# Distances of keys from TensorE for the one-hot rows of a product-key stage, and a tail of two stages

## The chip, the cores and the metric

The kernel runs on one core of a Trainium2 chip. The metric is the device time of one execution in microseconds (us), from the first to the last instruction with the launch around it; lower is better. Engines: TensorE (PE, its weight loads PEld), VectorE (DVE), ScalarE (ACT), GpSimd (POOL), and SyncE (SP), which here issues every DMA.

## The reference

256 tokens of width 1024 pass through three blocks: pooling with retention, a chunked linear recurrence (HGRN), and a block that joins RWKV-7 and latent attention. Each is followed by a product-key expert layer ("PEER"). The last steps are a per-layer embedding with a gate, and an RMS norm.

```python
def peer_ffn(h, w_q, sub_keys, expert_u, expert_v):      # per block of 128 tokens
    q = (hb @ w_q).reshape(n, HEADS, 2, 128)
    s = einsum('nhcd,hckd->nhck', q, sub_keys)
    sc, ix = top_k(s, 16)                                 # 16 of 128 keys on each side
    cand = sc[:, :, 0, :, None] + sc[:, :, 1, None, :]
    top, pos = top_k(cand.reshape(n, HEADS, 256), 16)     # expert = 128 * first key + second key
    eidx = ...
    gate = softmax(top)
    act = gelu(einsum('nhed,nd->nhe', expert_u[eidx], hb))
    return einsum('nhe,nhed->nd', gate * act, expert_v[eidx])

x = x + peer_ffn(rmsnorm(x, g_ffn), ...)                  # third of the three PEER layers
x = x + (p @ w_ple_proj) * sigmoid(rmsnorm(x, g_ple) @ w_ple_gate)
return rmsnorm(x, g_final)
```

## The kernel before, in words

**Experts without a gather.** `peer` (L430) does not gather. It multiplies all tokens with all 16384 experts, 128 at a time, and weights each product with a gate that is zero where the expert was not chosen. For one token the 128x128 table of gates is a product of two matrices over the 128 choices (8 heads x 16): row n of A holds the choice's weight at its first key, and row n of B holds 1 at its second key. G = A^T B.

**The select part.** TensorE makes queries and key scores (L568, L579), ScalarE copies them out, and VectorE finds the top 16 on either side and of the pairs (`halves`, `pairs`, `store`). Beside this, TensorE multiplies the first 16 rows of the u table, whose high and low parts ScalarE and GpSimd split (`early_scores`, banks 6 and 7 of PSUM). The four residual matmuls (L626), which start the accumulation in banks 0 to 3, stand between the last keys and the early scores 6 to 15. VectorE then leaves in `c.sel` the first keys, the second keys and the weights, tokens on partitions. TensorE transposes all three (L634) to `c.selt`, choices on partitions.

**The gates.** The 256 tokens go in 64 quads of four. For quad g:

- VectorE makes A in four `tensor_scalar` (L920): iota equal to the key of the choice, times its weight. A lies in four buffers, which are `c.h`.
- B is made by turns, after the string `MAKER`: by VectorE in one `tensor_tensor` (L917, letter D), by GpSimd in four `tensor_scalar` (L1005, P), or by ScalarE in four Abs and one Relu (L751, L754, A).
- TensorE multiplies the four pairs (L652) into bank 4 + g % 4. A wait on `dve_moved` keeps it from a bank that is not yet emptied.
- ScalarE copies 112 columns of each token to G (L760). VectorE multiplies the other 16 into `held`, the activations that the early scores left (`gate_held`, L910), two quads behind.

SP loads v rows 0 to 2 before this, one of them into `c.spare`. After the last quad but one is gated, TensorE does the first scores of the long loop, and then the held outputs (`output_tile`, L606), for which VectorE and ScalarE split `held` and the v rows (L769, L932 to L936). ScalarE's `held_high(1)` writes `vh[:, 1]`, which is the memory of the second half of `c.h`. The loop over the remaining 112 rows follows.

**The clock of stages.** Each `stage(...)` is a block: all engines finish it before any starts the next one. Loads given to `c.prefetch` are issued by SP at the start of the next stage, and `first_tile` waits for them.

**The tail.** After the third `peer` (`second_block`, L2723) nine stages follow: `take_banks` (L1011), a load of `pt`, `product` (L1180) for the projection, `rms_scale` (L1705) and `transposes` (L132) within `rms_t`, `product_split` (L1052) for the gate in high and low parts, `ple_add`, `rms_scale` again with `g_final`, and "store" in `program` (L2860), one DMA of 1 MB. `bank_rms_t` (L356), which "ffn" uses ahead of the third `peer`, takes the result straight from the PSUM banks, normalises it and transposes it in one stage; with `parts` it also splits it.

## Time and profile before

| | us |
|---|---|
| three runs | 3599.66, 3605.85, 3606.47 (median 3605.85) |
| the profiled execution | 3602.7 |
| its span | 3600.9 |
| mean granted TensorE clock in it | 0.963 of full |
| PE busy | 3307.2 (92%) |
| DVE busy | 2393.6 (66%) |
| ACT busy | 1527.1 (42%) |
| POOL busy | 423.5 (12%) |

The span runs from the first to the last instruction; the profiled execution's own time is 1.8 us longer, and what is worked out from rows refers to that one execution. A line of the timeline is: start, length, engine, source line, operation, output <- input, partitions x elements, type, count of instructions merged, and in brackets the idle time before with what ended it. The length of merged instructions runs from the first start to the last end. An f32 matmul leaves two records, each of its 128 or 512 columns; a matmul of type fp32r leaves one. In "64*128 64x256" the stationary operand has 64 rows and 128 columns and the moving one 256 columns. "PEq L105" is the start of a stage.

### The profile page before, as it was taken

The page shows a single profiled execution, that of the slowest core. Times are in us where ns is not written, and L with a number is a line of the kernel's source. Part 1 is how long each engine was busy: PE and PEld are TensorE (multiplying, and loading weights), DVE is VectorE, ACT ScalarE, POOL GpSimd, SP SyncE. Part 2 cuts the span into 40 slices and gives each one's busy share as a digit, 9 for nine tenths or more (in the row PEclk, how much of TensorE's full clock was granted, in tenths as well). Part 3 has the DMA queues.
Part 4 walks back from the last instruction along what each step waited for, and adds up shares of the span by engine and source line. Part 5 has one row for each costly group of instructions (what it writes and reads, how often), then busy time and mean ns, then how long its engine had stood idle before and what let it go on. Part 6 is the DMA issues. An engine that isn't in the chain of part 4 may idle for free. (4 is left out here: it accounts for less than half of the span.)

```text
span 3600.9 us, 59103 instructions
## 1 busy us (share of the span) xinstructions
PE 3307.2 (92%) x20776; PEld 2889.9 (80%) x20776; DVE 2393.6 (66%) x4940; ACT 1527.1 (42%) x2375; POOL 423.5 (12%) x460
## 2 busy tenths in 40 slices
PE   6888999999988797999999988988898899999995
PEld 5776899999986586799999976667587789999994
DVE  4699666666656589766666665555569866666663
ACT  3337444444444326544444443332424644444443
POOL 0257000000000048200000000000026500000000
PEclk9999999999998799999999998999999999999998
DMA  5320555555543231355555544100141155555552
GB/s 205 152 77 13 187 186 186 186 186 186 186 158 143 82 117 43 118 188 186 187 186 188 185 173 152 52 1 17 78 164 65 56 189 187 186 187 186 186 186 85
DMA packets 126992, 511.75 MB, mean 142 GB/s; under 512 B 14608, under 2 KB 15504, under 8 KB 119440
## 3 DMA queue, kind: packets, MB, share of 16 engines
q1 hardware_dynamic: 126864, 510.09, 39.7%
q8 instruction: 75, 1.23, 0.1%
q14 instruction: 53, 0.43, 0.0%
HBM read 508.99 MB, written 1.05 MB: 142 GB/s over the span
## 5 line engine op out<-in xcount | busy, mean ns | idle before, releaser
L588 PE MATMUL ps<-xh,uhigh 128*128 128x256 f32 x3072 | 869.6, 283 | 0.0
L590 PE MATMUL ps<-xh,ulow 128*128 128x256 f32 x3072 | 869.3, 283 | 0.0
L589 PE MATMUL ps<-xl,uhigh 128*128 128x256 f32 x3072 | 869.2, 283 | 0.0
L588 PEld LDWEIGHTS ps<-xh,uhigh 128*128 128x128 f32 x3072 | 588.3, 192 | 14.1 <-issue 0.7
L589 PEld LDWEIGHTS ps<-xl,uhigh 128*128 128x128 f32 x3072 | 588.3, 192 | 13.6 <-issue 0.7
L590 PEld LDWEIGHTS ps<-xh,ulow 128*128 128x128 f32 x3072 | 588.3, 191 | 0.0
L715 ACT CAST uhigh<-stream 128x1024 fp32r<-128x1024 f32 x336 | 352.7, 1050 | 471.2 <-DMA stream<-in_u 471.2
L941 DVE TENSOR_TENSOR ulow<-stream,uhigh 128x1024 fp32r<-128x1024 f32 x330 | 404.4, 1225 | 222.3 <-ACT uhigh L715 222.2
L606 PE MATMUL ps<-vhigh,chigh 128*128 128x512 f32 x1536 | 480.0, 394 | 2.9 <-DVE vlow L957 2.6
L606 PE MATMUL ps<-vlow,chigh 128*128 128x512 f32 x1536 | 475.9, 391 | 0.0
L606 PE MATMUL ps<-vhigh,clow 128*128 128x512 f32 x1536 | 474.5, 390 | 0.0
L946 DVE TENSOR_TENSOR stream<-stream,big 128x256 f32<-128x256 f32 x336 | 218.0, 649 | 383.6 <-ACT stream L775 383.6
L957 DVE TENSOR_TENSOR vlow<-stream,vhigh 128x1024 fp32r<-128x1024 f32 x336 | 409.5, 1219 | 8.5 <-ACT vhigh L783 8.5
L775 ACT ACTIVATE stream<-ps 128x256 f32<-128x256 f32 x336 | 129.1, 384 | 624.2 <-PE ps L590 624.2
L977 POOL TENSOR_TENSOR ulow<-stream,uhigh 128x1024 fp32r<-128x1024 f32 x39 | 96.3, 2476 | 2326.3 <-ACT uhigh L705 2301.9
L783 ACT CAST vhigh<-stream 128x1024 fp32r<-128x1024 f32 x336 | 350.3, 1042 | 10.0 <-DMA stream<-in_v 10.0
L606 PEld LDWEIGHTS ps<-vlow,chigh 128*128 128x128 f32 x1536 | 288.4, 188 | 64.2
L606 PEld LDWEIGHTS ps<-vhigh,clow 128*128 128x128 f32 x1536 | 288.4, 188 | 62.9
L606 PEld LDWEIGHTS ps<-vhigh,chigh 128*128 128x128 f32 x1536 | 263.9, 190 | 44.0 <-issue 10.5
L652 PE MATMUL ps<-stream 128*128 128x128 f32 x1536 | 226.4, 293 | 56.6 <-DVE stream L920 51.1
L652 PEld LDWEIGHTS ps<-stream 128*128 128x128 f32 x1536 | 191.6, 197 | 92.0 <-DVE stream L920 91.8
L1005 POOL TENSOR_SCALAR stream<-consts,stream 128x128 f32<-128x128 f32 x384 | 249.3, 664 | 28.2 <-PE ps L652 22.6
(487 smaller groups left out, 4354.9 us busy)
## 6 DMA issues: line engine op xcount, KB each, us to landing
stream<-in_u SPq DMA_DIRECT2D x369, 512.0 KB, 4.3
stream<-in_v SPq DMA_DIRECT2D x369, 512.0 KB, 3.5
big<-in_wq SPq DMA_DIRECT2D x24, 1152.0 KB, 6.6
stream<-in_ab_w_in SPq DMA_DIRECT2D x4, 2048.0 KB, 11.1
stream<-in_c_w_qf SPq DMA_DIRECT2D x16, 512.0 KB, 3.5
stream<-in_c_w_ig SPq DMA_DIRECT2D x4, 2048.0 KB, 8.1
big<-in_w_gates SPq DMA_DIRECT2D x4, 2048.0 KB, 7.8
spare<-in_u SPq DMA_DIRECT2D x15, 512.0 KB, 3.6
```

The lines of the kernel that those rows point to most:

```text
L588: pe.matmul(out, high[:, cols], c.xh[:, k, :], start=k == 0, stop=False)
L589: pe.matmul(out, high[:, cols], c.xl[:, k, :], start=False, stop=False)
L590: ins = pe.matmul(out, low[:, cols], c.xh[:, k, :], start=False, stop=k == KD - 1)
L606: ins = pe.matmul(c.ps[:, 2 * tt + half, :], left[:, b, tok], right[:, b, half * BANK:(half + 1) * BANK], start=False, stop=False, skip_gr ...
L652: ins = pe.matmul(c.ps[:, 4 + b, q * P:(q + 1) * P], A[:, b, q, :], B[:, b, q, :], start=True, stop=True)
L715: act.copy(uh[:, b], u[:, b]).then_inc(uh_ready, 1)
L775: act.activation(actv[:, b], c.ps[:, 4 + b, 0:T], ACT.Gelu).then_inc(gelu_ready, 1)
L783: act.copy(vh[:, b], v[:, b]).then_inc(vh_ready, 1)
L941: dve.tensor_tensor(ul[:, b], u[:, b], uh[:, b].bitcast(F32), ALU.subtract).then_inc(u_split, 1)
L946: dve.tensor_tensor(actv[:, b], actv[:, b], gate, ALU.mult).then_inc(ch_ready, 1)
L957: dve.tensor_tensor(vl[:, b], v[:, b], vh[:, b].bitcast(F32), ALU.subtract).then_inc(v_split, 1)
L1005: ins = pool.tensor_scalar(B[:, g % 4, q, :], c.iota[:], c.selt[:, 1, t:t + 1], None, ALU.is_equal)
```

## The change

In `peer`, VectorE's four instructions for A become one. Its input is a PSUM bank in which TensorE keeps, for choice n, token q of the quad and key j, the number key(n, q) - j. A is 0 == distance, times weight (`scalar_tensor_tensor`). TensorE keeps this bank up to date by adding, for each quad, the difference between the first keys of its tokens and those of the quad before: the stationary operand is `c.sel_r`, the first keys with tokens on partitions, in fp32r; the moving operand is four columns of `c.steps_r` (identity less the identity shifted by four), each repeated 128 times. One chain covers 64 tokens, half of the partitions, so a pair of quads takes two matmuls of 64 rows, on opposite halves, into banks 6 and 7. Only at the start of each 128 tokens is -j added, from `c.shares_r` and `c.iota_r`. The order of tokens follows: even quads walk the first 64 tokens of a tile, odd quads the second 64 (`token`).

The rest goes with it. A moves to the first half of `c.h` and to `c.spare`, products to banks 2 to 5. Residual matmuls of the second tile move behind the quads. The third v load waits for the last quad. `gate_held` is four quads behind, in pairs. B is made by VectorE in 5 of 16 quads, by GpSimd in 7 and by ScalarE in 4, where it was 2, 8 and 6. The first keys are no longer transposed. TensorE waits for the last gelu of the early scores before the first distances, since these take their banks.

In the tail, `bank_rms_t` does what three stages did, with the projection's matmuls between its own (`between`), and one stage "ple_gate" holds the gate product, sigmoid, addition, norm and store, by quarters of the result; the store goes out in two halves. The gate's weights go to `c.big`, `pt` and the projection's weights are loaded at the end of the third `peer` (`last`). The title of the change also names a join of the decays with the latent attention; the diff has no line on it.

```diff
         def _(pe):
+            if between is not None:
+                first_tile(c, pe, TABLES)
+                pe.wait_ge(h_ready, 1)
+                between(pe, 0)
             turn_tiles(c, pe, xn, xn_ready, turned)
+            if between is not None:
+                pe.wait_ge(h_ready, 2)
+                between(pe, 1)
...
-    MAKER = "DPAPAPAP"
-    made = lambda g: sum(MAKER[x % 8] == MAKER[g % 8] for x in range(g + 1))
+    MAKER = "DPAPDPAPDPADPAPD"
+    maker = lambda g: MAKER[g % len(MAKER)]
+    made = lambda g: sum(maker(x) == maker(g) for x in range(g + 1))
+
+    def token(g):
+
+        return g // 32 * P + g % 2 * (P // 2) + g % 32 // 2 * 4
...
-    A = c.h.rearrange("p t n -> p (t n)").rearrange("p (b q n) -> p b q n", b=4, q=4)
+    A = [x.rearrange("p (q n) -> p q n", q=4) for x in (c.h[:, 0, 0:BANK], c.h[:, 0, BANK:D],
+                                                        c.spare[:, 0:BANK], c.spare[:, BANK:D])]
...
             for n in range(3):
+                if n == 2:
+                    sp.wait_ge(g_ready, QUADS)
                 sp.dma_start(held_v[n], v_dram[n]).then_inc(held_v_landed[n], 16)
...
+            if last:
+                sp.wait_ge(held_vl, HELD)
+                sp.wait_ge(u_split, STEPS)
+            for slot, dst, src in last:
+                sp.dma_start(dst, src).then_inc(c.first_landed[slot], 16)
+                c.first_count[slot] += 16
...
-            for n in range(4):
-                ins = pe.matmul(c.ps[:, n, :], residual, c.h[:, n // 2, (n % 2) * BANK:(n % 2 + 1) * BANK],
-                                start=True, stop=False, skip_group_check=True)
-            ins.then_inc(res_done, 1)
+            def residual_tile(tt):
+                for half in range(2):
+                    ins = pe.matmul(c.ps[:, 2 * tt + half, :], residual, c.h[:, tt, half * BANK:(half + 1) * BANK],
+                                    start=True, stop=False, skip_group_check=True)
+                return ins
+
+            residual_tile(0).then_inc(res_done, 1)
             for n in range(6, HELD):
                 early_scores(n)
-            for s in range(3):
-                pe.wait_ge(keys_ready, 1 if s < 2 else 2)
+            def distances_of(m):
+
+                first = m % 16 == 0
+                for x in range(2):
+                    rows = slice(x * P // 2, (x + 1) * P // 2)
+                    t = token(2 * m + x)
+                    ins = pe.matmul(c.ps[:, 6 + x, :], c.sel_r[rows, t // P, :],
+                                    bc(c.steps_r[rows, t % P:t % P + 4], 2, P),
+                                    start=first, stop=False, skip_group_check=True)
+                if first:
+                    for x in range(2):
+                        rows = slice(x * P // 2, (x + 1) * P // 2)
+                        ins = pe.matmul(c.ps[:, 6 + x, :], c.shares_r[rows, :], bc(c.iota_r[rows, :], 1, 4),
+                                        start=False, stop=False, skip_group_check=True)
+                ins.then_inc(dist_ready, 1)
+
+            pe.wait_ge(keys_ready, 1)
+            pe.wait_ge(early_gelu, HELD)
+            distances_of(0)
+            for x in range(2):
+                pe.wait_ge(keys_ready, 1 + x)
                 for tt in range(NT):
-                    ins = pe.transpose(c.ps[:, 4 + s // 2, (s % 2) * T + tt * P:(s % 2) * T + (tt + 1) * P],
-                                       c.sel[:, s, tt, :], c.ident[:])
-                if s:
-                    ins.then_inc(turned, 1)
+                    ins = pe.transpose(c.ps[:, 4 + x, tt * P:(tt + 1) * P], c.sel[:, 1 + x, tt, :], c.ident[:])
+                ins.then_inc(turned, 1)
 
             for g in range(QUADS):
                 b = g % 4
+                if g % 2 and g + 1 < QUADS:
+                    pe.wait_ge(a_ready, g + 1)
+                    distances_of((g + 1) // 2)
                 pe.wait_ge(a_ready, g + 1)
-                if MAKER[g % 8] == "A":
+                if maker(g) == "A":
                     pe.wait_ge(act_b_ready, made(g))
-                elif MAKER[g % 8] == "P":
+                elif maker(g) == "P":
                     pe.wait_ge(b_ready, made(g))
-                if g < 4:
-                    if b >= 2:
-                        pe.wait_ge(early_gelu, HELD - 3 + b)
                 else:
+                    pe.wait_ge(own_ready, made(g))
+                if g >= 4:
                     pe.wait_ge(dve_moved, g - 3)
                 for q in range(4):
-                    ins = pe.matmul(c.ps[:, 4 + b, q * P:(q + 1) * P], A[:, b, q, :], B[:, b, q, :],
+                    ins = pe.matmul(c.ps[:, 2 + b, q * P:(q + 1) * P], A[b][:, q, :], B[:, b, q, :],
                                     start=True, stop=True)
                 ins.then_inc(g_ready, 1)
...
-            pe.wait_ge(dve_moved, QUADS - 2)
+            pe.wait_ge(dve_moved, QUADS - 1)
+            residual_tile(1).then_inc(res2_done, 1)
...
             def held_high(n):
                 act.wait_ge(held_v_landed[n % 3], 16 * (n // 3) + 16)
+                if n == 1:
+                    act.wait_ge(res2_done, 1)
...
-            dve.sem_inc(keys_ready, 1)
+            dve.tensor_copy(c.sel_r, c.sel[:, 0]).then_inc(keys_ready, 1)
...
-            for g in range(QUADS):
+            for g in range(0, QUADS, 2):
                 if g >= 4:
-                    dve.wait_ge(g_ready, g - 3)
-                if MAKER[g % 8] == "D":
-                    dve.tensor_tensor(B[:, g % 4], bc(c.iota, 1, 4), bc(c.selt[:, 1, 4 * g:4 * g + 4], 2, P), ALU.is_equal)
-                for q in range(4):
-                    t = 4 * g + q
-                    ins = dve.tensor_scalar(A[:, g % 4, q, :], c.iota[:], c.selt[:, 0, t:t + 1], c.selt[:, 2, t:t + 1],
-                                            ALU.is_equal, ALU.mult)
-                ins.then_inc(a_ready, 1)
-                if g >= 2:
-                    gate_held(g - 2)
-            gate_held(QUADS - 2)
-            gate_held(QUADS - 1)
+                    dve.wait_ge(g_ready, g - 2)
+                for x in (g, g + 1):
+                    if maker(x) == "D":
+                        t = token(x)
+                        dve.tensor_tensor(B[:, x % 4], bc(c.iota, 1, 4), bc(c.selt[:, 1, t:t + 4], 2, P), ALU.is_equal
+                                          ).then_inc(own_ready, 1)
+                if g >= 4:
+                    gate_held(g - 4)
+                    gate_held(g - 3)
+                dve.wait_ge(dist_ready, g // 2 + 1)
+                for x in (g, g + 1):
+                    t = token(x)
+                    dve.scalar_tensor_tensor(A[x % 4], c.ps[:, 6 + x % 2, :].rearrange("p (q n) -> p q n", q=4), 0.0,
+                                             bc(c.selt[:, 2, t:t + 4], 2, P), ALU.is_equal, ALU.mult).then_inc(a_ready, 1)
+            for g in range(QUADS - 4, QUADS):
+                gate_held(g)
...
-    peer(c, "peer2", d["wq2"], d["u2"], d["v2"], c.ident,
-         lambda: weight_loads(c, d["w_ple_proj"], 512, nk=2))
-    take_banks(c, "peer2_out")
-    a.at = 0
-    pt = a.tiles(2, T)
-    proj = a.take(NT * D).rearrange("p (t n) -> p t n", t=NT)
-    gate = a.take(NT * D).rearrange("p (t n) -> p t n", t=NT)
-    load(c, "ple_in", [(pt, d["pt"])])
-    product(c, "ple_proj", d["w_ple_proj"], 2, 512, proj, nk=2, lhs=pt, loaded=True)
-    c.prefetch(weight_loads(c, d["w_ple_gate"], 512))
-    rms_t(c, "ple", "g_ple", parts=(c.xh, c.xl))
-    product_split(c, "ple_gate", d["w_ple_gate"], 2, gate, 8192, func=ACT.Sigmoid, loaded=True)
-    chain = c.sem("ple_dve")
-    with stage(c, "ple_add") as block:
+    w_proj, pt = c.ring[:, 0:2 * D].rearrange("p (n k e) -> p n k e", n=2, k=2), c.spare[:, 0:2 * T].rearrange("p (k t) -> p k t", k=2)
+    peer(c, "peer2", d["wq2"], d["u2"], d["v2"], c.ident, lambda: ple_loads(c, d),
+         last=[(TABLES, pt, d["pt"])] + [(TABLES, w_proj[:, n].rearrange("p k e -> p (k e)"), d["w_ple_proj"][n])
+                                          for n in range(2)])
+    ple(c, d, pt, w_proj)
+
+
+def ple_loads(c, d):
+    W = c.big[:, 16384:16384 + 2 * KD * BANK].rearrange("p (n m) -> p n m", n=2)
+    return {**{n: [(W[:, n], d["w_ple_gate"][n])] for n in range(2)},
+            2: [(c.big[:, 0:D], d["g_final"].partition_broadcast(P))]}
+
+
+def ple(c, d, pt, w_proj):
+    W = c.big[:, 16384:16384 + 2 * KD * BANK].rearrange("p (n k m) -> p n k m", n=2, k=KD)
+    wh, wl = c.split_w("ple_gate", 8192)
+    g_row = c.big[:, 0:D]
+    gate = c.big[:, D:3 * D].rearrange("p (t n) -> p t n", t=NT)
+    part = c.big[:, 3 * D:4 * D].rearrange("p (x m) -> p x m", x=2)
+    junk = c.big[:, 4 * D:6 * D].rearrange("p (x m) -> p x m", x=4)
+    ss, rs = c.small[:, 0:4], c.small[:, 4:6]
+    out_bank = (lambda n, tt: 4 + 2 * tt + n)
+
+    def project(pe, tt):
+        for n in range(2):
+            for k in range(2):
+                ins = pe.matmul(c.ps[:, 2 * tt + n, :], pt[:, k, tt * P:(tt + 1) * P], w_proj[:, n, k, :],
+                                start=k == 0, stop=k == 1)
+        return ins
+
+    bank_rms_t(c, "ple", "g_ple", parts=(c.xh, c.xl), between=project)
...
+            highs(0)
+            highs(1)
+            gate_out(0)
+            gate_out(1)
+            square(0)
+            square(1)
+            gate_out(2)
+            square(2)
+            gate_out(3)
+            square(3)
+            act.wait_ge(summed, 1)
...
+            def add(u):
+                n, tt = UNITS[u]
+                cols = slice(n * BANK, (n + 1) * BANK)
+                dve.wait_ge(gated, u + 1)
+                link(dve.tensor_tensor(part[:, u % 2], c.ps[:, 2 * tt + n, :], gate[:, tt, cols], ALU.mult))
+                dve.tensor_tensor(c.h[:, tt, cols], c.h[:, tt, cols], part[:, u % 2], ALU.add).then_inc(added, 1)
+
+            lows(0)
+            lows(1)
+            for u in range(4):
+                add(u)
+            dve.wait_ge(squared, 4)
+            dve.tensor_reduce(rs, ss.rearrange("p (t n) -> p t n", t=NT), AX.X, ALU.add).then_inc(summed, 1)
+            dve.wait_ge(rooted, 1)
+            link(dve.reciprocal(rs, rs))
+            first_tile(c, dve, 2)
+            for tt in range(NT):
+                dve.scalar_tensor_tensor(c.h[:, tt, :], c.h[:, tt, :], rs[:, tt:tt + 1], g_row, ALU.mult, ALU.mult
+                                         ).then_inc(scaled, 1)
...
+            for k in range(KD):
+                pe.wait_ge(low_ready, k + 1)
+                for tt in range(NT):
+                    ins = block_of(0, tt, k)
+                ins.then_inc(chunk_done, 1)
+            for tt in range(NT):
+                for k in range(KD):
+                    pe.wait_ge(low_ready, KD + k + 1)
+                    ins = block_of(1, tt, k)
+                ins.then_inc(done, 1)
+
+        @block.sync
+        def _(sp):
+            for tt in range(NT):
+                sp.wait_ge(scaled, tt + 1)
+                sp.dma_start(d["out"][:, tt], c.h[:, tt]).then_inc(stored, 16)
...
+                act.copy(c.iota_r, c.iota)
...
+                dve.tensor_scalar(c.shares_r, c.iota, 0.0, -2.0 / P, ALU.mult, ALU.add)
+                dve.tensor_copy(c.steps_r[:, 0:4], c.ident[:, 0:4])
+                dve.tensor_tensor(c.steps_r[:, 4:P], c.ident[:, 4:P], c.ident[:, 0:P - 4], ALU.subtract)
...
-        stored = c.sem("stored")
-        with stage(c, "store") as block:
-            @block.sync
-            def _(sp):
-                sp.dma_start(out, c.h).then_inc(stored, 16)
-                sp.wait_ge(stored, 16)
```

## Rows read from the trace of the kernel before

**Rows 1.** The page, its first line.

```profile
span 3600.9 us, 59103 instructions
```

**Rows 2.** L652, TensorE, first `peer`: count, ns min/median/max, first and last start.

```profile
L652 PE MATMUL ps<-stream x512: 274/275/583, 258.5 to 350.2; 128*128 128x128 f32 x171
```

**Rows 3.** Windows of the first burst: length, busy PE, PEld, DVE, ACT, POOL, clock, DMA, GB/s.

```profile
258.50:350.40 91.90, 75.13 (x514) 63.74 (x515) 86.36 (x322) 72.91 (x178) 80.74 (x125) 0.98 0.00 1
```

**Rows 4.** Waits, 266 to 346 us: waiter, releaser, us in total, times, longest.

```profile
PEld ps L652 <- DVE stream L920: 25.9, 56, 1.0
```

**Rows 5.** Timeline inside the first burst: start, length, engine, line, operation.

```profile
313.64 2.60 POOL L1005 TENSOR_SCALAR stream<-consts,stream 128x128 f32<-128x128 f32 x4 [0.15 <-PE ps L652]
...
314.91 0.27 DVE L910 TENSOR_TENSOR big<-big,ps 128x64 f32<-128x64 f32 x1
...
315.08 0.69 DVE L917 TENSOR_TENSOR stream<-consts,stream 128x512 f32<-128x512 f32 x1
...
315.69 1.21 DVE L920 TENSOR_SCALAR stream<-consts,stream 128x128 f32<-128x128 f32 x4
...
316.82 0.26 DVE L910 TENSOR_TENSOR big<-big,ps 128x64 f32<-128x64 f32 x1
```

**Rows 6.** Timeline of TensorE in the tail.

```profile
3525.99 0.61 PE L606 MATMUL ps<-vhigh,clow 128*128 128x512 f32 x2
...
3557.23 0.80 PE L1115 MATMUL ps<-ple_gate_high,xh 128*128 128x512 f32 x1 [4.87 <-DVE ple_gate_low L1097]
...
3581.66 0.39 PE L1115 MATMUL ps<-ple_gate_high,xl 128*128 128x512 f32 x1
```

**Rows 7.** Timeline of SyncE's queue in the tail.

```profile
3596.59 0.34 SPq L2893 DMA_DIRECT2D out<-stream  x1
```

**Rows 8.** Timeline of VectorE in `rwkv_tile`, a PSUM source.

```profile
2311.49 0.68 DVE L2383 TENSOR_TENSOR stream<-ps,stream 128x512 f32<-128x512 f32 x1
```

**Rows 9.** Timeline of TensorE in `rwkv_tile`, 128x128 f32 back to back.

```profile
2317.10 2.84 PE L2227 MATMUL ps<-stream 128*128 128x128 f32 x24
```

**Rows 10.** Groups by shape in `rwkv_tile`, 2308.7 to 2312 us: busy, mean ns, idle.

```profile
L2227 PE MATMUL ps<-big 64*128 64x256 f32 x16 | 2.0, 387 | 0.9 <-PEq L105 0.9
```

**Rows 11.** Timeline of TensorE in the RWKV stage, 2235.6 to 2243 us.

```profile
2235.60 1.99 PE L1907 MATMUL ps<-big 64*128 64x256 f32 x8
2237.52 1.98 PE L1925 MATMUL ps<-big,stream 128*128 128x512 f32 x4
2239.34 1.88 PE L1913 MATMUL ps<-stream,big 128*128 128x512 f32 x4
2241.06 1.88 PE L1925 MATMUL ps<-big,stream 128*128 128x512 f32 x4
2242.87 1.99 PE L1907 MATMUL ps<-big 64*128 64x256 f32 x8
```

**Rows 12.** Waits, 205 to 250 us, ahead of the first burst.

```profile
PEld ps L634 <- DVEq L893: 3.7, 1, 3.7
```

**Rows 13.** L626, the residual matmuls of three calls; columns as in rows 2.

```profile
L626 PE MATMUL ps<-stream,consts x24: 592/592/697, 213.5 to 2718.8; 128*128 128x512 f32 x24
```

**Rows 14.** Timeline of the stage "ffn", which `bank_rms_t` makes.

```profile
2620.62 2.36 DVE L389 COPY stream<-ps 128x1024 f32<-128x1024 f32 x2 [9.93 <-PEq L105]
...
2625.68 3.73 PE L223 MATMUL ps<-consts,big 128*128 128x128 f32 x16 [5.50 <-DVE big L394]
...
2629.44 0.69 DVE L399 TENSOR_TENSOR stream<-ps,cols 128x512 f32<-128x512 f32 x1 [0.16 <-PE ps L223]
```

**Rows 15.** DMA issues: count, size of each, us to landing.

```profile
stream<-in_w_ple_gate SPq DMA_DIRECT2D x2, 2048.0 KB, 10.6
```

**Rows 16.** Windows, the start of the gate product; columns as in rows 3.

```profile
3557.00:3563.00 6.00, 5.77 (x14) 4.57 (x15) 4.99 (x9) 3.96 (x8) 0.00 (x0) 0.50 0.00 0
```

**Rows 17.** The chain that ended last: start, length, what.

```profile
3590.70 1.28 ACT L1717
...
3593.97 2.29 DVE stream L1734
```

73 lines of the change are left out of this document (57 added, 16 removed).

## The prediction

> **What bounds the kernel now.** The page first: one core, a span of 3600.9 us [rows 1]. The diff touches two places, so I read those two stretches and leave out the long loops over the tables.
>
> The first place is the stage inside each of the three `peer` calls that turns the chosen keys into gates. Its matmuls (L652) stand in three bursts; the line view shows the first, from 258.5 to 350.2 us [rows 2]; the other two last as long. That is 91.7 us for 64 groups of four tokens ("quads"), or 1.43 us a quad. The windows view shows all four engines busy, none full: VectorE 86.4, GpSimd 80.7, TensorE 75.1, ScalarE 72.9 of 91.9 us, at full clock nearly throughout, and no DMA [rows 3]. The waits decide: TensorE's weight loads wait for VectorE's line L920, the one-hot operand A [rows 4]. In the timeline one quad of A (four `tensor_scalar`) takes VectorE 1.13 us from start to the next start, `gate_held` (L910) 0.17, and the B operand that VectorE makes once in eight quads (L917) 0.61 [rows 5]. 1.13 + 0.17 + 0.61/8 = 1.38 of the 1.43 us. VectorE is the bound.
>
> The second place is the tail. The last table matmuls end at 3526.6; the gate product runs from 3557.2 to 3582.05; the end is 3600.9 [rows 1, 6]. That is 74.3 us in nine stages, one engine after the other, with a store of 1 MB that starts at 3596.6 and costs 4.3 us [rows 7].
>
> **Part 1: the quads.** Removed from VectorE: 4 `tensor_scalar` a quad. Added: one `scalar_tensor_tensor` of 128x512 with the distances from PSUM. The trace has none of that size. Its nearest row is a `tensor_tensor` of 128x512 from PSUM and SBUF, 0.68 us [rows 8], like L917's 0.69, whose start to start is 0.61 [rows 5]; I take 0.61. Upper bound: half rate, 1.15; lower: none under 0.5. VectorE also makes B in 5 of 16 quads, not 2. A pair of quads is then 2x0.61 + 2x0.17 + 0.61x5/8 = 1.94 us, with four waits of about 0.1 some 2.3, or 1.15 a quad. No longer the bound.
>
> TensorE pays. Its own pace for the A x B matmuls is not the 1.43 seen: 24 records of the same 128x128 f32 form take 2.84 us elsewhere, (2.84 - 0.28)/23 = 0.111 each, and a quad has 8: 0.89 us [rows 9]. Added for each pair are two fp32r matmuls of 64 rows and 512 columns, one on each half of the array's rows. Two such matmuls of 128 rows take 0.61 us, the last 0.39 of it, so 0.22 to 0.23 each [rows 6]. Do the halves run side by side? 16 records of 64x256 whose rows alternate between the halves take 2.0 us, about 0.11 each [rows 10]; eight of the same form on one half take 1.92, or 0.21 each without the overhead below [rows 11]. They do, and I take 0.23 for the two, bounds 0.23 and 0.45.
>
> Going from 128 rows to 64 and back costs. In the timeline the starts are 1.92, 1.82, 1.72 and 1.81 us apart; all four runs hold as many columns, and the one that touches no change of shape takes 1.72. So the 64-row run pays 0.20, each neighbour 0.1: 0.4 us an excursion [rows 11]. The Trainium skill, TensorEngine Tiling (Array Packing), Key Properties, states that changing the tiling mode drains TensorE, while tiles of one mode run in parallel; the trace agrees with both halves. By the parallel half alone a pair would be 0.4 us shorter; the sum goes by the rows.
>
> A pair on TensorE: 2x0.89 + 0.23 + 0.40 = 2.41 us. The chain must fit too: distances end, their result lands (0.2), VectorE makes A (0.68), the load starts (0.1), about 1.0 us, while the quad that covers it is 0.89 long. I add 0.1 to 0.2. GpSimd makes B in 7 of 16 quads at 2.6 us each [rows 5], 1.14 a quad on average, yet in quads 1 to 9 it has every second one, 1.30 or more. So 2.64 us a pair, **1.32 a quad**, 84.5 us: 7.2 saved. Bounds: 1.18 (GpSimd's average with its gaps, changes of shape hidden) and 1.45 (halves in turn, loads exposed). ScalarE drops from 24 to 16 groups of keys out of its 72.9 us [rows 3] and stays below. Quad 32 restarts the sums with two more matmuls, 0.2 us, in the rounding.
>
> **Around the quads.** The first A comes sooner, one 0.61 for 1.13: 0.5 saved. The cast of the keys (0.3) on VectorE lies where it waits for ScalarE's exponential anyway; nothing, 0.3 if that cover goes. The first distances run before the transposes, in TensorE's idle time. Half of the residual matmuls move behind the quads. Ahead they cost nothing (TensorE then waited 3.7 us for VectorE's keys [rows 12]); behind, each is two records of 512 columns [rows 13], 0.43 to 0.45 from start to start [rows 11], so two matmuls 1.75 us, plus 0.2 for waiting on one more gate. Queued behind them are the first scores and all held outputs: **1.95 lost**. The third held v is loaded after the last quad, not before the first; it is needed some 7 us later and lands in about 3.5, so nothing. ScalarE's wait for the residual before the second `held_high` ends before TensorE has finished the first scores. Nothing.
>
> Per peer: -7.2 - 0.5 + 1.95 = -5.75; three: **-17.3 us**. The start stage gains three short VectorE operations, some 0.5 us, while the next one waits for its weights: nothing, at most 0.5.
>
> **Part 2: the tail.** The banks go through `bank_rms_t`. As "ffn" it runs from 2620.6 to 2630.1, 9.5 us [rows 14]; with the split (another cast and subtraction of one group) 10.9, with the stage's start and end 11.8: from 3526.6 to 3538.4. TensorE multiplies the ple projection in between (4 f32 matmuls a tile, 8 x 0.43 = 3.4 us) while it would wait 5.1 us for the first normalised tile [rows 14]; covered at full clock, 1.7 us late at half clock. The gate weights are now asked for at 3527 and not at 3543, into memory that the tables have left. Landing took 10.6 us [rows 15], so 3538 to 3540: just in time, up to 1.5 us late. On SP their issues, and those of `g_final`, stand ahead of nothing.
>
> First high and low 1.4 us, then the product. Before it took 24.8 us, the first 6 at half clock, the 0.50 of that window [rows 6, 16]; TensorE now comes in busy, so 96 x 0.23 = 22 to 22.5: done at 3562.3. What follows is work on the last quarter: sigmoid 0.6, multiply and add 0.7 each, square 0.8, sum 0.2, table load and root 1.6, reciprocal 0.2, two scalings of 1024 at 1.25, waits 0.3, and a store of 512 KB, 3.6. These are estimates cut to size from the chain's rows (1.28 for the table, 2.29 for 2048 elements on VectorE [rows 17]) and from the 4.3 us of the store [rows 7]: 11.2 us where 18.9 stood. End at 3573.5: **-27.4 us**, bounds -21 and -30. The proj and pt loads of `peer2` wait for the last splits; queued behind them on SP is nothing.
>
> **Sum.** The profiled execution took 3602.7 us (span 3600.9). 3602.7 - 17.3 - 27.4 = **3558**. That execution lies 3.2 us below the median of the three runs, 3605.85, and between its ends; I keep its base.
>
> **Rivals.**
> *GpSimd is the only bound.* The changes of shape hide behind weight loads, the pace falls to 1.18: 75.5 us, -14.75 a peer, 3531. For it: GpSimd is the second busiest engine of the burst [rows 3]. Against: the changes of shape show their price in the open [rows 11].
> *TensorE is the new bound at the old pace*: halves in turn or loads exposed, 1.45, 92.8 us, +2.55 a peer, 3583. Here belongs the port rule: the Trainium skill, SBUF — State Buffer, Who interferes with whom, states that a VectorE instruction with two SBUF inputs and a GpSimd one that reads SBUF lock each other out. As a mechanism of this kernel: VectorE's 20 B operands a burst would wait up to one GpSimd instruction of 0.65 us, 6.5 us in the mean, which uses up the slack. Against it: L917 took 0.69 us inside a GpSimd stretch [rows 5].
> *Slower: the new VectorE instruction runs at half rate.* Place: a PSUM source with a broadcast second operand. Price 1.15 for 0.61: a pair is 2.30 + 0.34 + 0.38 + 0.25 = 3.27, 1.63 a quad, 104.6 us, +14.35 a peer, 3618. It decides from 1.55 a quad on (3 x (64r - 90.25) = 27.4). Against: a two-input instruction with the same source takes no longer than one from SBUF [rows 8, 5].
> *The change doesn't do what it says.* The title speaks of joining the decays with the latent attention; the diff holds nothing of that, so it brings nothing. What could fail is the overlap in the tail: if the projection and late weights hold everything, it saves 10, 3575.
>
> **How the numbers follow.** Forecast (1.24 to 1.40 a quad, 3545 to 3572) 0.55; GpSimd bound 0.18; old pace 0.19; half rate 0.04; weak overlap 0.04. The range takes in the weak overlap, half of the GpSimd case and most of the old pace: 3532 to 3586. A measurement of this kernel can tell about 0.2%, 7 us. Beyond that on the fast side lie nearly all cases: 0.92. Within it: an old pace with a poor tail, 0.04. Slower: half rate, 0.04.
>
> **What would show it.** L652's burst 84 us long; its loads waiting for VectorE in short stretches; the `scalar_tensor_tensor` at 0.68; the two 64-row matmuls starting at the same time; 0.2 us gaps on either side of them; 1.75 us of residual behind the burst; the last table matmul to the end in 47 us; the gate product at clock 1.0. Wrong if the burst is under 78 or over 90 us, if the new VectorE line takes over 1 us, or if the product starts after 3542 less what the peers saved.

## The result, and the profile after

The kernel after takes **3551.11 us** (median of 4 runs, 3548.56 to 3556.06), the kernel before 3606.16 us beside it (4 runs, 3599.66 to 3609.69). The ratio is 0.9851, 95% interval 0.9832 to 0.987. The forecast was 3558 in a range of 3532 to 3586.

The profiled execution of after took 3553.21 us. Its first line, for [rows 1]:

```profile
span 3551.4 us, 58703 instructions
```

The span is 49.5 us shorter. Followed from anchor to anchor (us, the three peers in turn; a burst is taken from the start of its first A x B record to the start of its last, and what follows from there):

| stretch | before | after | change | forecast |
|---|---|---|---|---|
| start to the first query matmul | 129.1 | 130.2 | +1.1 | 0 |
| first query matmul to first quad | 129.4, 128.4, 128.5 | 125.8, 126.4, 126.6 | -7.6 | -1.5 |
| the burst of quads | 91.7, 91.6, 91.7 | 84.0, 85.1, 83.8 | -22.0 | -21.6 |
| last quad to first held output | 3.2, 3.2, 3.2 | 5.0, 5.0, 5.0 | +5.3 | +5.85 |
| held outputs to the next queries, or to the last output | 895.9, 1157.9, 672.3 | 898.4, 1158.3, 671.5 | +2.0 | 0 |
| start of the last table matmul to the end | 74.7 | 46.4 | -28.3 | -27.4 |

The forecasts for the burst, for what follows it and for the tail hold. That for the select part does not: it gained five times what I gave it. The +2.0 comes from one stretch of this one execution: from the first held output of peer 0 to the first query of peer 1 it took 898.4 us, and 894.4 to 896.5 in all twelve experiments below.

**The burst.** L652 is now L696. Its row for the first peer, for [rows 2]:

```profile
L696 PE MATMUL ps<-stream x256: 274/275/582, 256.0 to 338.0; 128*128 128x128 f32 x128
L696 PE MATMUL ps<-stream,spare x256: 275/275/377, 260.5 to 340.0; 128*128 128x128 f32 x128
```

The window over that burst, columns as in [rows 3]:

```profile
256.00:340.30 84.30, 82.06 (x576) 68.20 (x576) 65.39 (x145) 58.80 (x138) 68.73 (x109) 0.97 0.00 1
```

VectorE fell from 86.4 of 91.9 us to 65.4 of 84.3. TensorE, busy 82.1, is now the busiest engine. Its records overlap, so this share does not by itself say that nothing else lengthens the burst. The waits from 264 to 338 us, where before TensorE waited 25.9 us for VectorE [rows 4]:

```profile
ACT big L805 <- PE ps L696: 18.0, 27, 1.2
PEld ps L696 <- issue: 10.7, 40, 0.4
POOL stream L1056 <- PE ps L696: 9.8, 12, 1.3
DVE stream L974 <- PE ps L662: 5.8, 11, 0.5
...
PEld ps L696 <- DVE spare L974: 0.5, 3, 0.2
```

Three engines wait for TensorE, and TensorE hardly for VectorE. But its weight loads sit idle 40 times for a cause that the profile does not name ("issue"). The timeline of two pairs shows which (for [rows 5]):

```profile
306.47 0.72 ACT L799 ACTIVATE stream<-stream,consts 128x512 f32<-128x512 f32 x1
...
307.26 0.97 PEld L696 LDWEIGHTS ps<-stream,spare 128*128 128x128 f32 x8 [0.36 <-issue]
...
308.35 0.48 PE L662 MATMUL ps<-steps_r,first_keys 64*128 64x512 f32 x2
...
308.76 1.16 PE L696 MATMUL ps<-stream,spare 128*128 128x128 f32 x8
308.87 1.29 DVE L974 SCALAR_TENSOR_TENSOR stream<-ps,stream 128x512 f32<-128x512 f32 x2 [0.53 <-PE ps L662]
...
310.74 0.48 PE L662 MATMUL ps<-steps_r,first_keys 64*128 64x512 f32 x2
...
311.69 0.72 ACT L799 ACTIVATE stream<-stream,consts 128x512 f32<-128x512 f32 x1
...
312.48 0.97 PEld L696 LDWEIGHTS ps<-stream,spare 128*128 128x128 f32 x8 [0.36 <-issue]
...
313.57 0.48 PE L662 MATMUL ps<-steps_r,first_keys 64*128 64x512 f32 x2
```

L662 is the distances, L799 the Relu that ends ScalarE's B, L974 VectorE's A. Two distance matmuls of 0.48 together last 0.48: the halves start at once. From one excursion (the two 64-row matmuls between those of 128 rows) to the next it is 2.39 us (308.35 to 310.74), then 2.83 (to 313.57). 2.39 is the forecast's TensorE pair of 2.41. In the longer pair the load that waits (312.48) starts 0.07 us after ScalarE's Relu (L799) ends at 312.41, and the same stands at 307.19 and 307.26. The 40 idle times are 28 of 0.23 us right behind the distances, one of 0.35 behind the restart of the sums (L668), and 11 of 0.36 us, each of which ends 0.07 us after a Relu. So these pairs seem to wait for ScalarE's B.

The period from one pair of distances to the next holds the second quad of one pair and the first quad of the next. In the steady part of the three bursts its median is 2.83 us where ScalarE makes the B of that first quad, 2.64 where it makes that of the second quad, and 2.39 otherwise. ScalarE has quads 2, 6, 10 and 13 of 16, so half of the periods are long.

**Ahead of the burst.** VectorE and ScalarE at the end of the first select part, after:

```profile
245.61 1.05 ACT L760 CAST uhigh<-stream 128x1024 fp32r<-128x1024 f32 x1 [5.48 <-DMA stream<-in_u]
...
248.17 1.28 ACT L788 ACT_TABLE_LOAD   x1
...
248.91 1.91 DVE L940 CAST first_keys<-stream 128x256 fp32r<-128x256 f32 x1
...
251.47 1.84 DVE L945 TENSOR_TENSOR stream<-stream,big 128x256 f32<-128x256 f32 x1
```

The exponential (L788) that VectorE's weights need stands in ScalarE's queue behind casts of u rows, and those wait for a DMA. Its table load came 121.1, 120.2 and 120.3 us behind the first query before, and 118.0, 118.6 and 118.8 after.

**The tail.** TensorE after, for [rows 6, 14], and the end, for [rows 7, 17]:

```profile
3505.02 0.39 PE L628 MATMUL ps<-vhigh,clow 128*128 128x512 f32 x1
3507.22 3.67 PE L2810 MATMUL ps<-stream,spare 128*128 128x512 f32 x8 [1.81 <-DVE stream L396]
3510.91 1.09 PE L223 MATMUL ps<-consts,big 128*128 128x128 f32 x8
3512.67 1.09 PE L223 MATMUL ps<-consts,big 128*128 128x128 f32 x8 [0.67 <-ACT big L387]
3513.60 3.60 PE L2810 MATMUL ps<-stream,spare 128*128 128x512 f32 x8
3518.98 0.50 PE L2891 MATMUL ps<-ple_gate_high,xh 128*128 128x512 f32 x1 [1.78 <-DVE ple_gate_low L2863]
...
3540.64 0.39 PE L2891 MATMUL ps<-ple_gate_high,xl 128*128 128x512 f32 x1
...
3543.89 1.28 ACT L2854 ACT_TABLE_LOAD   x1
...
3545.71 2.48 DVE L2883 SCALAR_TENSOR_TENSOR stream<-stream,small,big 128x1024 f32<-128x1024 f32 x2
3547.03 1.54 SPq L2910 DMA_DIRECT2D out<-stream  x2
```

The first stage ends with TensorE at 3517.20, 11.8 us behind the last table matmul's end at 3505.41 (forecast 11.8). The gate product lasts from 3518.98 to 3541.05, 22.07 us, all at full clock (forecast 22 to 22.5). 10.3 us follow (forecast 11.2).

### The profile page after: what moved, and what is told of

Its sections match the earlier page's. It is cut to its first block and busy times, and to the rows that moved or that the text cites. A ratio compares the mean times of both kernels' runs of the same rounds, so it can differ in the third digit from the quotient of the medians.

```text
span 3551.4 us, 58703 instructions
## 1 busy us (share of the span) xinstructions
PE 3327.6 (94%) x20974; PEld 2901.9 (82%) x20974; DVE 2329.5 (66%) x4413; ACT 1485.1 (42%) x2257; POOL 387.8 (11%) x412
## 5 line engine op out<-in xcount | busy, mean ns | idle before, releaser
L1056 POOL TENSOR_SCALAR stream<-consts,stream 128x128 f32<-128x128 f32 x336 | 212.6, 650 | 40.8 <-PE ps L696 36.2
L590 PE MATMUL ps<-stream,big 128*128 128x256 f32 x768 | 174.1, 388 | 4.9 <-PEq L105 4.9
L590 PEld LDWEIGHTS ps<-stream,big 128*128 128x128 f32 x768 | 148.8, 195 | 26.7 <-issue 6.0
```

Of the source, the lines that this page charges most:

```text
L590: ins = pe.matmul(c.ps[:, h % 2, half * T:(half + 1) * T], W[:, h % SLOTS, half * QW + k * P:half * QW + (k + 1) * P], c.xt[:, k, :], star ...
L1056: ins = pool.tensor_scalar(B[:, g % 4, q, :], c.iota[:], c.selt[:, 1, t:t + 1], None, ALU.is_equal)
```

## Experiments

The theory from the traces: (a) the tail and the quads are independent gains; (b) in the burst TensorE sets the pace, and ScalarE's B (its "keys") lengthens about every second pair; (c) the select part is shorter because residual matmuls were taken out of the chain that ends in the exponential, which the forecast had called free. The rivals: VectorE's chain sets the burst, and VectorE's search for keys sets the select part. Where "bursts" has one number below, it is the mean of the three; six profiles with the burst code of after (after, e1, e5, e6, e11, e12) give 84.5 us.

**e1: the quads alone.** `second_block` keeps the tail of before.

```diff
-    ple(c, d, pt, w_proj)
+    take_banks(c, "peer2_out")
...
+    product_split(c, "ple_gate", d["w_ple_gate"], 2, gate, 8192, func=ACT.Sigmoid, loaded=True)
...
```

> The changed select stages with the tail of before. The prediction's steps are independent of each other, so this one should keep only what the three peers gained: the trace of after has its last output matmul 21.2 us earlier than before, so about 3606 - 21 = 3585 us (my terms as written gave 17.3 less, 3589). If the two halves help each other (the tail's new stages shift what the last peer's stretch waits for), it is outside 3581 to 3589.

Measured 3581.17 us (5 runs, before 3605.11), ratio 0.9936 [0.9922, 0.9949]: -23.9 us. Tail 74.5, bursts 84.5. That is at the fast end of what was expected (3581 to 3589).

**e2: the tail alone.** `peer` as before, with `last`, `ple_loads` and `ple`.

```diff
-                                            bc(c.selt[:, 2, t:t + 4], 2, P), ALU.is_equal, ALU.mult).then_inc(a_ready, 1)
+                    ins = dve.tensor_scalar(A[:, g % 4, q, :], c.iota[:], c.selt[:, 0, t:t + 1], c.selt[:, 2, t:t + 1],
+                                            ALU.is_equal, ALU.mult)
```

> The select stages of before with the new tail. Theory: the tail's 28.3 us are its own, so about 3606 - 28 = 3578 us, and the profile shows the gate product 22 us long at the full clock and the end 46 us behind the last output. Rival: the tail's product runs at full clock only because of what the new select stages leave before it; then the product is longer than 22 us and the gain under 24 us.

Measured 3575.2 us, ratio 0.992 [0.9906, 0.9933]: -29.9 us; tail 46.4. The two sum to -53.8, the change brought -55.0: independent, as far as these measurements can tell. The rival is out: the product runs as in after, and the gain is over 24 us.

**e3: distances over all 128 rows.** The column of `steps_r` that starts the second half is made a pure identity, so the sums are the same.

```diff
-                    ins = pe.matmul(c.ps[:, 6 + x, :], c.sel_r[rows, t // P, :],
-                                    bc(c.steps_r[rows, t % P:t % P + 4], 2, P),
+                    ins = pe.matmul(c.ps[:, 6 + x, :], c.sel_r[:, t // P, :],
+                                    bc(c.steps_r[:, t % P:t % P + 4], 2, P),
```

> After, with the two distance matmuls of a pair over all 128 rows, one behind the other, in place of two 64-row halves side by side. Theory (the prediction's 0.4 us per excursion is the price of changing the array's row grouping): a TensorE-bound pair goes from 2.41 us to 2 x 0.89 + 2 x 0.23 = 2.24 us; with 32 pairs a burst, of which half are held by ScalarE's keys and keep their time, the burst is 2 to 5 us shorter, 6 to 15 us in all (about 3540 us). Rival: the grouping costs nothing by itself and the 0.4 us is the latency of the keys behind; then each pair pays 0.23 us more for the second matmul, up to 7 us a burst, about 3565 to 3573 us.

Measured 3549.05 us, ratio 0.9844 [0.9831, 0.9858]; bursts 81.6, 83.1, 82.2. The intervals of after and e3 overlap, so the times alone show nothing; the bursts are 2.2 us shorter. TensorE in e3:

```profile
308.28 0.68 PE L660 MATMUL ps<-steps_r,first_keys 128*128 128x512 f32 x2
308.80 1.05 PE L693 MATMUL ps<-stream,spare 128*128 128x128 f32 x8
309.74 1.16 PE L693 MATMUL ps<-stream 128*128 128x128 f32 x8
310.65 0.68 PE L660 MATMUL ps<-steps_r,first_keys 128*128 128x512 f32 x2
...
313.33 0.46 PE L660 MATMUL ps<-steps_r,first_keys 128*128 128x512 f32 x1
```

The free pair is 2.37 us, not the 2.24 of the theory, and not the 2.6 of the rival. So doing the halves one behind the other costs what doing them together and changing shape costs. In after the pair holds 2.39 - 2 x 0.89 - 0.23 = 0.38 us beyond its matmuls, in e3, where the shape never changes, 2.37 - 2 x 0.89 - 2 x 0.23 = 0.13. So by this difference the change of shape costs 0.25 us, as much as a second matmul. The pairs held by ScalarE fell from 2.83 to 2.68; why, no run isolates.

**e4: ScalarE makes its keys one group sooner.**

```diff
+            if maker(2) == "A":
+                act_keys(2)
             for g in range(QUADS):
-                if maker(g + 2) == "A" and g + 2 < QUADS:
-                    act_keys(g + 2)
+                if maker(g + 3) == "A" and g + 3 < QUADS:
+                    act_keys(g + 3)
```

> After, with ScalarE making its key groups three groups ahead of the copy it stands behind instead of two. Theory: every second pair of the burst is 2.83 us instead of 2.39 because TensorE waits for ScalarE's keys; without that wait all pairs are about 2.4 us, the burst about 5 us shorter (79 instead of 84), 15 us in all, about 3536 us. Rival 1: the pace is set by the chain through VectorE (comparison, gate products), which then ends last; the burst gets under 2 us shorter. Rival 2: ScalarE's keys now delay its own copy, VectorE gets its products later, and the burst is as long or longer (3551 to 3556 us).

Measured 3543.43 us, ratio 0.9833 [0.9819, 0.9846]; bursts 80.9, 81.5, 80.4. The burst is 3.6 us shorter where the theory had 5, the median 7.7 us less where it had 15: the theory's direction, and part of its size. The interval overlaps after's [0.9832, 0.987], so the proof is in the bursts: none of these three is above 81.6 us, none of the 18 with after's code below 83.7. TensorE and the waits of e4:

```profile
307.24 0.48 PE L662 MATMUL ps<-steps_r,first_keys 64*128 64x512 f32 x2
...
309.63 0.48 PE L662 MATMUL ps<-steps_r,first_keys 64*128 64x512 f32 x2
...
312.27 0.48 PE L662 MATMUL ps<-steps_r,first_keys 64*128 64x512 f32 x2
```

```profile
DVE big L959 <- ACT big L807: 8.2, 11, 1.0
...
PEld ps L696 <- issue: 6.7, 29, 0.3
...
PEld ps L696 <- DVE spare L976: 1.7, 10, 0.2
```

These are the waits from 264 to 336 us. Of the 40 idle times the 11 behind a Relu are gone and the other 29 are left. The long pair is 2.64 us now, no longer 2.83, and the pair whose second quad is ScalarE's went from 2.64 to 2.39. The rest of its length has moved: VectorE's gate products wait 8.2 us for ScalarE's copies (4.2 in after), which stand behind a group of keys. Rival 1 holds for this rest; its "under 2 us" was too little.

**e5: the first tile's residual matmuls behind the early scores.**

```diff
-            residual_tile(0).then_inc(res_done, 1)
             for n in range(6, HELD):
                 early_scores(n)
+            residual_tile(0).then_inc(res_done, 1)
```

> After, with the two residual matmuls of the first tile moved from ahead of the early scores 6 to 15 to behind them, where TensorE waits for the keys. Theory: they stand in the chain that ends the select part (early scores, their gelu on ScalarE, then the exponential that stands behind it in ScalarE's queue, the weights on VectorE), so each peer's first quad comes 1.75 us sooner, 5.2 us in all, about 3546 us. Rival (the prediction's own step, that ahead they cost nothing): VectorE's search for the keys ends the select part and nothing moves, 3551 us.

Measured 3546.03 us (before 3604.94), ratio 0.9842 [0.9828, 0.9855]. The select part fell to 124.8, 125.0 and 124.7 us, 1.7 less than the 126.5 that seven profiles with the unchanged select part of after average (after, e1, e3, e4, e7, e11, e12). The interval overlaps after's; the stretch shows the gain. In the first peer the exponential itself was late, at 118.5, and 1.5 us came back behind it, for a reason of its own (last section). Over the four profiles that hold this edit (e5, e8, e9, e10) the exponential comes at 117.0 us, against 118.7 in the seven, and the first quad at 124.6, against 126.5. The theory holds, by its 1.75.

**e6: the second tile's residual ahead too, as in before.**

```diff
-            residual_tile(0).then_inc(res_done, 1)
+            residual_tile(0)
+            residual_tile(1).then_inc(res_done, 1)
```

> After, with the two residual matmuls of the second tile also issued ahead, as in the kernel before (they are done once more behind, where they start the sums anew, so the result does not change). Read in the profile from the first query matmul to the first quad. Theory: 1.75 us more in each peer. Rival (the prediction): no change.

One run, 3556.51 us. The exponential's table load came 120.4, 119.9 and 119.8 us behind the first query, where after has 118.0, 118.6 and 118.8 and e5, with none ahead, 118.5, 117.2 and 116.9. The first quads followed at 128.2, 126.2 and 127.6. Two more matmuls ahead cost 1.3 us up to the exponential against the mean of the seven profiles (118.7), and 1.6 against after alone; in one peer the next stretch gave 1.5 back, as in e5.

**e7: the makers of before.**

```diff
-    MAKER = "DPAPDPAPDPADPAPD"
+    MAKER = "DPAPAPAPDPAPAPAP"
```

> After, with the makers of B of the kernel before: VectorE 2 of 16 quads, GpSimd 8, ScalarE 6, where after has 5, 7 and 4. Theory: the burst of after is held in every second pair by ScalarE's keys, so 24 groups in place of 16 add 2 to 5 us to each burst (86 to 89 us in place of 84), 6 to 15 us in all, 3557 to 3566 us. Rival: TensorE's own pace of 2.4 us a pair sets the burst whoever makes B, and it stays 84 us, 3551 us.

Measured 3563.85 us (4 runs), ratio 0.9887 [0.9872, 0.9902]; bursts 88.2, 88.0, 87.2. The change of makers is worth 3.3 us a burst: without it the burst would have gained 3.8 us and not 7.1. With half as many again of ScalarE's groups the burst is longer by what the theory says. GpSimd's 32 groups are in this number too, but the periods part the two. Their medians (us), by who makes B in the two quads of a period:

| | after | e4 | e7 |
|---|---|---|---|
| the first quad of the next pair by ScalarE | 2.83 | 2.64 | 2.77 to 2.83 |
| the second quad of the pair by ScalarE | 2.64 | 2.39 | (none) |
| neither | 2.39 | 2.39 | 2.39 |

In e7 the second quad of every pair is GpSimd's, yet the periods that end in a quad with VectorE's B are 2.39 us, as in after; only those that end in one with ScalarE's are long, and there are six of them in eight. Of the waits from 264 to 342 us, 21 end 0.07 us after a Relu, where after had 11.

**e8: the three edits together** (e3, e4, e5).

> After, with the three edits together: the distances over all 128 rows, ScalarE's keys three groups ahead, the first tile's residual matmuls behind the early scores. If they add up: 3551 less 8 (keys ahead), less 2 to 6 (128 rows), less 5 (residual), 3532 to 3536 us. The bursts should be 78 to 79 us: 2 x 0.91 + 0.52 = 2.34 to 2.4 us a pair, 75 to 77, and the cold start of the first pairs. Rival: with ScalarE out of the way the 128-row form meets the chain through VectorE and brings nothing more, bursts 80 to 81, 3538 to 3542 us.

Measured **3535.86 us** (3534.55 to 3539.08), ratio 0.9812 [0.9799, 0.9826], the best complete version of the study; its interval lies clear of after's [0.9832, 0.987]. The time is in the theory's range. But the bursts are 81.3, 80.3 and 81.4, as in e4, and so are the periods, 2.66 and 2.38 us: the rival is right that the 128-row form brings nothing more once ScalarE is out of the way. The gain is e4's and e5's.

**e9: e8 with one ScalarE group in 16 given to VectorE.**

```diff
-    MAKER = "DPAPDPAPDPADPAPD"
+    MAKER = "DPAPDPAPDPDDPAPD"
```

> The version with three edits, with B of one more quad in 16 by VectorE and one fewer by ScalarE (6, 7 and 3 in place of 5, 7 and 4). Theory: what is left over TensorE's 2.37 us a pair comes from VectorE's gate products, which wait for ScalarE's copies standing behind a group of keys (8.2 us of waits in 73 of one burst); with 12 groups of keys a burst in place of 16 a quarter of it goes, 1 to 2 us a burst, 3 to 6 us in all, 3530 to 3533 us. Rival: VectorE, with 4 more B at 0.61 us, delays its own A by as much, and the time stays 3536 us or rises to 3538 us.

Measured 3538.29 us, the same ratio of 0.9812 [0.9799, 0.9826]; bursts 81.8, 81.1, 81.8. VectorE's waits for the copies fell from 8.2 to 6.5 us in the first burst, and the burst did not follow. The pair that now has two of VectorE's B takes 2.77 us, where e8 has 2.66: the rival is right.

**e10: e8 without most distance matmuls.** This leaves out the update of the first keys in 30 of 32 pairs of a burst.

```diff
-                    distances_of((g + 1) // 2)
+                    if (g + 1) // 2 % 16 == 0:
+                        distances_of((g + 1) // 2)
...
-                dve.wait_ge(dist_ready, g // 2 + 1)
+                dve.wait_ge(dist_ready, g // 32 + 1)
```

> The version with three edits, with the distance matmuls left out except at the start of each 128 tokens (the first keys of the other quads are wrong by that; everything else is done). It shows what TensorE pays for them and what bounds the burst next. Theory: without 0.52 us a pair TensorE would need 1.85 us a pair, 59 us a burst, so GpSimd is next, 28 groups at 2.6 us, 73 us and its waits: 74 to 76 us a burst, 5 to 6 less than the 81 of the version with three edits, about 3519 us. This is the pace of the prediction's rival (GpSimd the only bound, 1.18 us a quad, 75.5 us). Rival: the chain through ScalarE's copies and VectorE holds it at 79 to 81 us.

Measured 3523.99 us (4 runs), ratio 0.9768 [0.9753, 0.9783]; bursts 77.3, 77.7, 77.2. It lies between the two. Waits of e10 from 262 to 328 us:

```profile
PEld ps L694 <- DVE spare L974: 11.4, 14, 1.2
DVE big L957 <- ACT big L805: 10.5, 11, 1.5
POOL stream L1056 <- PE ps L694: 6.2, 9, 1.3
```

By these waits GpSimd is not next, since it still waits 6.2 us, but the chain from ScalarE's copies through VectorE's gate products to A. TensorE's 0.52 us a pair, 15.6 us a burst, were worth 3.6.

**e11: the tail without the projection's matmuls.** Their result is missing from the last sum.

```diff
-    bank_rms_t(c, "ple", "g_ple", parts=(c.xh, c.xl), between=project)
+    bank_rms_t(c, "ple", "g_ple", parts=(c.xh, c.xl))
```

> After, with the eight matmuls of the embedding's projection left out of the tail's first stage (the projected values are missing from the last sum, their loads stay). Theory as in the prediction: they lie in the time in which TensorE waits for the normalised tiles, so nothing or under 0.5 us, 3551 us, within what a measurement can tell. Rival: in the profile of after the second tile's four matmuls end within 0.2 us of the end of the stage, so the stage is as long as TensorE makes it, and ends 1 us or more sooner without them.

Measured 3554.46 us (4 runs), ratio 0.986 [0.9845, 0.9875]: no gain, and in the one profiled execution the tail is 48.6 us, **2.2 us longer with eight matmuls fewer**. TensorE in e11:

```profile
3511.00 3.73 PE L223 MATMUL ps<-consts,big 128*128 128x128 f32 x16 [5.50 <-DVE big L401]
3519.60 0.80 PE L2891 MATMUL ps<-ple_gate_high,xh 128*128 128x512 f32 x1 [4.87 <-DVE ple_gate_low L2863]
```

And the windows of e11 and of after, 3511 to 3517 and 3517 to 3523, columns as in [rows 3]:

```profile
3511.00:3517.00 6.00, 3.73 (x16) 3.14 (x16) 4.47 (x8) 3.92 (x7) 0.00 (x0) 0.50 1.01 434
3517.00:3523.00 6.00, 3.40 (x8) 2.73 (x9) 5.01 (x9) 4.64 (x9) 0.00 (x0) 0.50 0.27 112
```

```profile
3511.00:3517.00 6.00, 5.33 (x24) 3.03 (x24) 5.09 (x9) 3.63 (x6) 0.00 (x0) 1.00 1.00 426
3517.00:3523.00 6.00, 4.22 (x19) 3.34 (x19) 4.83 (x9) 5.31 (x10) 0.00 (x0) 1.00 0.27 112
```

Without the projection TensorE idles 5.5 us, the granted clock falls to 0.50 (1.2 GHz), the 16 transposes take 3.73 us and the first matmuls of the product run at half pace. With it the clock stays at 1.00 (2.4 GHz). The projection is more than covered: it pays. Of the eleven profiles that have it in this tail, ten show 46.4 us and one 48.0 (e9, last section).

**e12: the residual behind the quads done twice.**

```diff
+            residual_tile(1)
             residual_tile(1).then_inc(res2_done, 1)
```

> After, with the two residual matmuls behind the quads done twice (the second pair starts the sums anew, so the result does not change). From the last quad's first matmul to the first held output 5.0 us in after. Theory: they stand in the open, 1.75 us more, 6.7 us, and about 5 us more in the whole execution (3556 us). Rival: the first scores and the held outputs wait for something else (ScalarE's or VectorE's splits), and it stays 5.0 us.

One run, 3553.78 us. From the last quad to the first held output it took 6.7 us in all three peers, where after has 5.0: 1.7 more each. (Both count from the last record of the last quad; from its first record, which the expectation names, they are 7.5 and 5.8.) The theory holds there. The whole is up by 2.7 and not 5 on after's median; of one run that is no contradiction.

## Why the prediction was right, and where it was not

**The bound.** Right: VectorE's four instructions for A were it. The new one takes 0.682 us at the median and starts every 0.61, as taken from [rows 8] and [rows 5]; the half-rate rival is out.

**TensorE's pair, 2.41 us.** Measured 2.39 where nothing else holds it. Both halves start at once, as [rows 10] said. The 0.40 for the change of shape was right as a sum (0.38) and too much as a cause: 0.13 of it is left in e3, which changes no shape. The rule that I cited from the Trainium skill, TensorEngine Tiling (Array Packing), Key Properties, names both effects, the drain and the parallel tiles; the runs add that at this size they cancel.

**"I add 0.1 to 0.2", to 2.64 a pair.** The size was right (84.5 us forecast, 84.5 the mean of 18 bursts), the reason was not, so this was luck. 2.64 is 0.23 above 2.41, which is more than the 0.1 to 0.2; I put it on the chain from distances to A and on GpSimd's first quads. Measured, the steady pairs take 2.59 on average, from the medians above (half of them 2.39), and some 2 us a burst are lost in the first pairs. In after that chain just fits: distances start at 308.35, A's first half is done at 309.55, and TensorE needs it at 309.65. What lengthens half of the pairs is ScalarE's B, and the step that failed is "ScalarE drops from 24 to 16 groups of keys out of its 72.9 us [rows 3] and stays below". Its share of busy time is 58.8 of 84.3 us, but it makes a group only after the copy of a quad just done, so that the group comes late. e4 shows it by moving the group, e7 by adding some, and the periods say which pairs pay. What was taken for slack in a sum of busy time was none in the order of its queue.

**The select part: the mis-sized step.** "Ahead they cost nothing (TensorE then waited 3.7 us for VectorE's keys [rows 12])". Two of them cost 1.3 (e6) to 1.7 us a peer (e5, e8 to e10), shown from both sides, so some 5 us in all. (Over all profiles the select part is 128.7 us in before and e2 and 126.5 in the seven named under e5; 1.8 of the 2.2 lies ahead of the exponential, which came at 120.5 and 118.7.) With it the forecast would have been 3553. The wait in [rows 12] is real, but not the one that ends last: the weights come later than the keys, and behind them stand exponential, casts, the DMA of u rows, the buffers freed by early scores, and the matmuls ahead of these. That order of the chain is read from the code and the rows; the runs show its first and last link. One link more is in the rows: in all three peers of after the last step of the weights (L945) ends 0.3 us behind GpSimd's last split of u rows, which follows the last cast (last section). The 0.5 for the first A is about right: from the exponential's table load to the first quad 8.2 us before, 7.8 after.

**Behind the quads.** 1.95 forecast, 1.8 measured, and e12 doubles its main part.

**The tail.** -27.4 forecast, -28.3 measured. The gate weights, feared up to 1.5 us late, hold nothing: ScalarE's first cast starts at 3517.58, 0.4 us into its stage. The prediction called the projection "covered at full clock"; e11 shows that it is what makes the clock full.

**The base, and luck.** I worked from the profiled execution of 3602.7 us, 3.5 under the median of 3606.16 beside after. That error went the other way and hid a part of the miss: from the median the forecast would have been 3561.5. The terms saved 44.7 us; the medians differ by 55.0, so 10.3 were missed, and 6.9 of them show. Between the two profiled executions the change is 49.5 us, 4.8 more than forecast: 6.1 in the select part, 0.9 in the tail, 0.4 in the bursts and 0.5 behind them, less the 3.1 by which start and long loops were slower in this execution of after. The other 2.1 of the 6.9 is that this execution lies 2.1 above its median.

**The rivals.** GpSimd as the only bound (3531) is out: e10, without TensorE's share, still has 77.4 us and GpSimd waiting. The old pace (3583) is out. The lock that it named is there, but on GpSimd's side: L966 took 0.68 to 0.69 us in 57 of 60 cases, while each GpSimd instruction that started during it was held, 5.6 us a burst in all (last section). GpSimd had that to spare, since it still waits 9.8 us for TensorE. The row that the prediction set against the lock, L917 at 0.69 us, showed VectorE's side alone; in before, too, the 24 GpSimd instructions that started during L917 took 0.8 us or more.

## What to carry to other kernels

- An engine with 70% busy time can be the bound of every second step or so, when its order puts a slow item right before the one that is awaited. Read the period between two equal events, look for the period that is longer, and see what ends just before.
- A wait of some us on an engine does not make what stands ahead of it free. Ask which wait ends last, and whether what stands ahead frees a buffer for a DMA that this last wait needs.
- To find a lock between two engines, compare the durations of both: the one that came second shows it.
- Useful matmuls put in TensorE's idle stretch can save more than their own time, since the next product then starts at full clock.

## What was not expected of the hardware

**VectorE and GpSimd hold each other up, and the one that starts second pays.** In the select part GpSimd splits u rows by a `tensor_tensor`, and this is its row in after:

```profile
248.33 4.69 POOL L1028 TENSOR_TENSOR ulow<-stream,uhigh 128x1024 fp32r<-128x1024 f32 x2 [7.56 <-ACT uhigh L760]
```

L940, a cast of 128x256, took 0.29 us where it started ahead of GpSimd's, and 1.91 where it started behind it. L945 took 0.42 in e5's first peer, where it started together with GpSimd's second, and 1.84 in after's, which began behind it. And in e5 L966 took 1.52 once, beside GpSimd's last split, against 0.68 in the burst. L945 in after:

```profile
L945 DVE TENSOR_TENSOR stream<-stream,big x3: 1840/1840/2607, 251.5 to 2740.2; 128x256 f32<-128x256 f32 x3
```

Where L945 escapes, the exponential's table load to the first quad is 6.3 to 6.4 us and not 7.8 (e5's first peer, e6's and e8's second): that is the 1.5 us that e6 got back.

In the burst it is mostly GpSimd that pays. L966, VectorE's B with two SBUF inputs, and the GpSimd instruction that started 0.04 us behind it, in after:

```profile
307.25 0.68 DVE L966 TENSOR_TENSOR stream<-consts,stream 128x512 f32<-128x512 f32 x1
...
307.29 1.11 POOL L1056 TENSOR_SCALAR stream<-consts,stream 128x128 f32<-128x128 f32 x1
```

In after 48 of GpSimd's 336 `tensor_scalar` start while L966 runs. All 48 take 0.80 to 1.11 us and end 0.47 us behind it; the other 288 take 0.61 at most, beside L974 too, whose first input is in PSUM. L966 itself kept to 0.69 us where GpSimd's instruction had 0.37 us or less to go, and took 0.79 to 0.81 in the three cases with 0.48 or more to go. In e4 it did so more often:

```profile
308.96 0.83 DVE L968 TENSOR_TENSOR stream<-consts,stream 128x512 f32<-128x512 f32 x1
```

The Trainium skill, SBUF — State Buffer, Who interferes with whom, says that a VectorE instruction with two SBUF inputs contends with a GpSimd one that reads SBUF, that a cast can contend too, and that the order of issue decides who is held. The rows agree, in the select part and in the burst.

**A clock that falls within a product.** In the profiled execution of e9 the gate product, after the same work ahead of it as in after, ran at half pace from 3505.7 to 3509 us, and its tail was 48.0 us, not 46.4:

```profile
3502.00:3508.00 6.00, 4.22 (x13) 3.04 (x13) 4.83 (x9) 4.78 (x9) 0.00 (x0) 0.80 0.30 124
3508.00:3514.00 6.00, 6.00 (x26) 4.93 (x25) 3.43 (x6) 2.49 (x4) 0.00 (x0) 0.92 0.00 0
```

TensorE had just come through gaps of 0.66 and 1.78 us, in after through 0.67 and 1.78. So the full clock in the tail is likely (ten of eleven profiles), not certain, and 1.6 us hang on it.
